# A Mamba-2 scan on one NeuronCore: the state part of y from C scaled per head

## What is computed

```python
cb = einsum('bclgn,bcsgn->bclsg', Cm, Bm)
wts = cb[..., None] * decay * dt[:, :, None]
y_diag = einsum('bclsgr,bcsgrp->bclgrp', wts, x)
...
y_off = einsum('bclgn,bcgrpn,bclgr->bclgrp', Cm, h_prev, exp(acum))
y = (y_diag + y_off).reshape(b, L, SSD_HEADS, P)
```

## Time and profile before

| | us |
|---|---|
| median of 3 runs | 1295.1 |
| lowest, highest | 1293.67, 1297.56 |
| the profiled execution | 1294.7 |
| its span, first to last instruction | 1293.0 |
| PE busy | 1199.7 (93%) |
| DVE, ACT, POOL busy | 522.7, 410.7, 428.1 |
| mean granted clock of PE, share of full speed | 0.973 |

### The profile page before, as it was taken

One profiled execution on the slowest core, in us unless ns is written; L12 is line 12 of the kernel. 1 busy time (PEld: TensorE's weight loads), 2 busy tenths in 40 slices (PEclk: granted clock), 3 DMA queues, 4 the chain that ended last, 5 costly groups with the idle time before them and its releaser, 6 DMA issues.

```text
span 1293.0 us, 22479 instructions
## 1 busy us (share of the span) xinstructions
PE 1199.7 (93%) x8759; PEld 1040.4 (80%) x8759; DVE 522.7 (40%) x855; ACT 410.7 (32%) x690; POOL 428.1 (33%) x343
## 2 busy tenths in 40 slices
PE   5999999999998999999899999999997879887985
PEld 5999999999985997798698689999997645543542
DVE  5445442101645665484665561104344241130114
ACT  4211214343444454453444452222324100010112
POOL 6444432233424432452342343434330111213210
PEclk8999999999999999999999999999999899997999
DMA  6332322123510730451162132253638999999995
GB/s 159 78 82 74 81 78 66 53 82 82 147 50 18 189 82 17 119 135 50 53 169 66 33 106 72 76 136 108 204 106 310 387 401 403 407 402 392 403 370 173
DMA packets 185911, 207.51 MB, mean 160 GB/s; under 512 B 12781, under 2 KB 162669, under 8 KB 177354
## 3 DMA queue, kind: packets, MB, share of 16 engines
q1 hardware_dynamic: 175962, 187.42, 43.8%
q0 software_dynamic: 6048, 12.54, 3.5%
q10 hardware_dynamic: 3822, 6.39, 1.3%
HBM read 191.71 MB, written 26.20 MB: 169 GB/s over the span
## 4 chain that ended last, share of the span: by engine, by line
PE 80%; DMA 8%; DVE 4%; issue 3%; POOL 2%; ACT 2%; SPq 1%; ACTq 0%; DVEq 0%; POOLq 0%
PE acc L677 52%; PE pTS L1076 6%; PE acc L959 4%; PE acc L1120 3%; DMA area<-in_w_down 2%; DMA area<-in_w_up 2%; DMA ring<-in_w_gate 2%; PE pTS L859 2%; PE pY L853 2%; PE pY L877 1%; SPq L602 1%; PE pO L807 1%; PE acc L818 1%; DMA area<-in_w_down,area 1%; PE pO L827 1%
## 5 line engine op out<-in xcount | busy, mean ns | idle before, releaser
L677 PE MATMUL acc<-h_parts,ring_parts 128*128 128x328 f32 (+1 forms) x3840 | 543.1, 303 | 6.3 <-DVE area L1340 2.2
L677 PEld LDWEIGHTS acc<-h_parts,ring_parts 128*128 128x128 f32 x3840 | 532.3, 190 | 18.2 <-issue 11.5
L1993 POOL TENSOR_TENSOR ring_parts<-ring,ring_parts 128x1024 fp32r<-128x1024 f32 x112 | 280.8, 2507 | 494.2 <-ACT ring_parts L1691 494.1
L1691 ACT ACTIVATE ring_parts<-ring 128x1024 fp32r<-128x1024 f32 x112 | 118.8, 1060 | 379.5 <-PE acc L677 352.7
L1076 PE MATMUL pTS<-area,big 128*64 128x256 f32 x672 | 108.4, 406 | 17.9 <-DMA ring<-in_w_gate 6.2
L677 PE MATMUL acc<-u_parts,ring_parts 128*128 128x264 f32 (+1 forms) x640 | 109.4, 299 | 0.0
L1076 PEld LDWEIGHTS pTS<-area,big 128*64 128x64 f32 x672 | 68.2, 147 | 51.0 <-issue 12.5
L677 PEld LDWEIGHTS acc<-u_parts,ring_parts 128*128 128x128 f32 x640 | 96.4, 188 | 0.0
L677 PE MATMUL acc<-area_parts,ring_parts 128*128 128x264 f32 (+1 forms) x512 | 91.1, 299 | 0.0
L1296 DVE SCALAR_TENSOR_TENSOR area<-area,xvec 128x616 f32<-128x616 f32 x72 | 79.4, 1102 | 10.5 <-DVE area L1294 0.6
L677 PEld LDWEIGHTS acc<-area_parts,ring_parts 128*128 128x128 f32 x512 | 78.4, 188 | 0.0
(11 more groups left out here) (397 smaller groups left out, 1519.5 us busy)
## 6 DMA issues: line engine op xcount, KB each, us to landing
ring<-in_w_in SPq DMA_DIRECT2D x80, 512.0 KB, 4.0
area<-in_w_gate SPq DMA_DIRECT2D x20, 1024.0 KB, 20.9
area<-in_w_up SPq DMA_DIRECT2D x20, 1024.0 KB, 22.9
area<-in_w_down SPq DMA_DIRECT2D x20, 1024.0 KB, 21.2
area<-in_state_ssm SPq DMA_DIRECT2D x16, 512.0 KB, 6.9
out<-area SPq DMA_DIRECT2D x16, 512.0 KB, 5.4
ring<-in_w_ssd_out SPq DMA_DIRECT2D x16, 512.0 KB, 4.1
ring<-in_w_gate SPq DMA_DIRECT2D x7, 1024.0 KB, 16.8
```

The costliest lines, as they stand in the source:

```text
L677: m = nc.tensor.matmul(acc[a][:, h, 0:n], w[s][:, k, :], x[:, k, h * HALF:h * HALF + n], start=first and k == 0 and w is w_hi and x is hi, ...
L1691: a_.activation(w_hi[b % 2], w_raw[b % 2], ACT.Copy).then_inc(hi_done, 1)
L1993: gp.tensor_tensor(w_lo[b % 2], w_raw[b % 2], w_hi[b % 2].bitcast(F32), ALU.subtract).then_inc(lo_done, 1)
```

## The change

In tiles 0 to 3 the state part is no longer made with tokens on the partitions and turned back. C (128 state rows by 128 tokens) is multiplied by `exp(acum)` once per head, and eight matmuls, one per head, add state times these features right into `pY`, ahead of the batch with the weights. The factors lie along the tokens, so they have to stand on all 128 partitions: ACT makes `e_row` = exp of the running sums (32 heads by 592) once, SP writes it to DRAM (`e_rows`, one row per full tile), and in each full tile ACT issues two DMAs which read 512 numbers of a row (4 heads by 128 tokens) to all partitions, into `c_of`, in the place of the convolution's `raw` buffers. POOL then multiplies C in (`scale_c`) and signals PE (`s_ce`). L807, L1328 and L877 remain in tile 4 alone.

The core of the diff (in the full one `z_y` and `p_yo` give up their semaphores, and counts follow):

```diff
+        e_row = area[0:HEADS, at_pad + T:at_pad + 2 * T]
+        c_of = [raw[:, n, XH:XH + 4 * P] for n in range(2)]
+        e_rows = nc.dram_tensor("e_rows", [4, HEADS * P], F32).ap()
 # SP, ahead of the scan
-            sp.wait_ge(s_dta, 8)
+            sp.wait_ge(s_dta, 9)
+            for i in range(4):
+                sp.dma_start(e_rows[i].rearrange("(h c) -> h c", c=P), e_row[:, i * P:(i + 1) * P]).then_inc(ac_rows, 16)
...
-            sp.wait_ge(ac_rows, 32)
+            sp.wait_ge(ac_rows, 96)
 # PE
-                    pe.wait_ge(s_y1, g * 5 + (i + 1))
+                    if i == 0:
+                        pe.wait_ge(s_y1, g + 1)
+                    else:
+                        pe.wait_ge(s_cb, g * 5 + i)
+                        pe.wait_ge(s_bt, g * 5 + i)
...
-                    pe.wait_ge(s_cb, g * 5 + (i + 1))
-                    pe.wait_ge(s_bt, g * 5 + (i + 1))
-                    if i < 4:
-                        nc.tensor.matmul(pO[0:r, :], cT[:, tok(i)], st, start=True, stop=True).then_inc(p_yo, 1)
...
+                    pe.wait_ge(s_exp, g * 10 + (2 * i + 3))
+                    if i < 4:
+                        pe.wait_ge(s_ce, g * 4 + (i + 1))
+                        for h in range(HPG):
+                            half, at = head(h)
+                            nc.tensor.matmul(pY[half, at], st[:, h * HD:(h + 1) * HD], c_of[h // 4][:, h % 4 * P:(h % 4 + 1) * P],
+                                             start=h < 2, stop=False)
...
-                    pe.wait_ge(s_y1, g * 5 + (i + 2))
-                    for k in range(GK):
...
 # DVE
-                        dve.wait_ge(p_yo, g * 4 + (i + 1))
+                        dve.wait_ge(p_y, g * 5 + (i + 2))
...
-                    dve.wait_ge(p_yt, g * 5 + (i + 1))
+                    if i == 4:
+                        dve.wait_ge(p_yt, g + 1)
 # ACT, once, and in each tile between the copy of B and the exps
+            a_.activation(e_row, xT_new[0:HEADS, 0:T], ACT.Exp).then_inc(s_dta, 1)
...
+                    if i < 4:
+                        act.wait_ge(s_cvd, g * 6 + 8)
+                        act.wait_ge(ac_rows, 96)
+                        for q in range(2):
+                            act.dma_start(c_of[q], e_rows[i:i + 1, bass.ds(g * (HPG * P) + q * 4 * P, 4 * P)].broadcast_to([P, 4 * P])
+                                          ).then_inc(e_in, 16)
 # POOL
+                def scale_c(i):
+
+                    hold(pool, e_in, g * 128 + (32 * i + 32))
+                    for q in range(2):
+                        by_head = c_of[q].rearrange("p (h c) -> p h c", h=4)
+                        x = gp.tensor_tensor(by_head, by_head, cT[:, tok(i)].unsqueeze(1).broadcast_to([P, 4, P]), ALU.mult)
+                    x.then_inc(s_ce, 1)
+
+                hold(pool, s_silu, g * 6 + 8)
+                scale_c(0)
                 split_lo(g_block(g, 6), 6)
                 for i in range(1, TILES):
                     if i < 4:
+                        scale_c(i)
                         split_lo(g_block(g, 6 + i), 6 + i)
```

More of the change, by code:

```diff
@@ L329, in build @@
         s_hist, s_tail, s_cvd, s_silu = (sem(n) for n in ("s_hist", "s_tail", "s_cvd", "s_silu"))
-        p_xt, p_cb, p_seg, p_yo, p_y, p_sn, p_yt = (sem(n) for n in ("p_xt", "p_cb", "p_seg", "p_yo", "p_y", "p_sn", "p_yt"))
+        p_xt, p_cb, p_seg, e_in, p_y, p_sn, p_yt = (sem(n) for n in ("p_xt", "p_cb", "p_seg", "e_in", "p_y", "p_sn", "p_yt"))
         s_u, s_y1, s_xd, s_cb, s_bt, s_ac, s_exp, s_w, s_st = (
@@ L362, in build @@
                              "f_out", "f_skip"))
-        z_sd, z_y, y_out = (sem(n) for n in ("z_sd", "z_y", "y_out"))
+        z_sd, s_ce, y_out = (sem(n) for n in ("z_sd", "s_ce", "y_out"))
         def s_block(turn, b):
@@ L649, in _ @@
             for i in range(TILES):
-                sp.wait_ge(z_y, i + 1)
+                sp.wait_ge(s_htok, TILES + i + 1)
                 if i == 0:
@@ L792, in _ @@
                         if q == 0:
[L793 removed]
+                            pe.wait_ge(ac_rows, 96 + 16 * TILES * (g + 1))
                             pe.wait_ge(s_exp, g * 10 + (2 * i + 1))
@@ L851, in _ @@
                     for h in range(HPG):
-                        k, half = h // 2, slice(HD * (h % 2), HD * (h % 2) + HD)
-                        m = nc.tensor.matmul(pY[half, k * P:k * P + r], xdt[0:r, i % 2, h * HD:(h + 1) * HD],
-                                             wts[0:r, h // 4, (h % 4) * r:(h % 4 + 1) * r], start=h < 2, stop=False)
+                        half, at = head(h)
+                        m = nc.tensor.matmul(pY[half, at], xdt[0:r, i % 2, h * HD:(h + 1) * HD],
+                                             wts[0:r, h // 4, (h % 4) * r:(h % 4 + 1) * r], start=i == 4 and h < 2,
+                                             stop=i < 4 and h >= HPG - 2)
                     m.then_inc(p_y, 1)
                     kk = r if i < 4 else LASTP
-                    pe.wait_ge(s_exp, g * 10 + (2 * i + 3))
                     nc.tensor.matmul(pS[:, :], btok[0:kk, i % 2, :], xte[0:kk, i % 2, :], start=True, stop=True
@@ L863, in _ @@
                         pe.wait_ge(s_bm, g + 1)
-                        pe.wait_ge(s_y1, g * 5 + 6)
+                        pe.wait_ge(s_y1, g + 2)
                         def state_update(k):
@@ L873, in _ @@
                         state_update(1)
-                    pe.wait_ge(s_y1, g * 5 + (i + 2))
-                    for k in range(GK):
-                        m = nc.tensor.matmul(pY[:, k * P:k * P + r], ytok[0:r, k * P:(k + 1) * P], ident[0:r, 0:r],
-                                             start=False, stop=k == GK - 1)
-                    m.then_inc(p_yt, 1)
+                        pe.wait_ge(s_y1, g + 2)
+                        for k in range(GK):
+                            m = nc.tensor.matmul(pY[:, k * P:k * P + r], ytok[0:r, k * P:(k + 1) * P], ident[0:r, 0:r],
+                                                 start=False, stop=k == GK - 1)
+                        m.then_inc(p_yt, 1)
                 pe.wait_ge(s_st, g * 6 + 6)
@@ L1269, in _ @@
             v.tensor_scalar(da.rearrange("p i h -> p (i h)"), pY[:, 0:160], -1.0, None, ALU.mult).then_inc(s_ac, 1)
-            dve.wait_ge(s_dta, 8)
+            dve.wait_ge(s_dta, 9)
             v.memset(arow.bitcast(F32), 0.0).then_inc(s_ac, 1)
@@ L2080, in _ @@
                     if i < 4:
+                        scale_c(i)
                         split_lo(g_block(g, 6 + i), 6 + i)
                     if i == 1:
-                        hold(pool, s_silu, g * 6 + 8)
                         gp.tensor_copy(cmask[:, 0:LASTP], cT[:, 4 * P:TP])
```

13 lines of the change are left out of this document (8 added, 5 removed).

## The result

The changed kernel takes 1331.0 us (median of 4 runs, 1328.4 to 1332.9) against 1296.3 us before on the same chip, a ratio of 1.027 with a 95% interval of 1.0242 to 1.0298. The forecast was 1308 us with a range up to 1320: the sign is right and the size is not, 35 us instead of 13. The profiled execution took 1331.9 us, 37.2 more than that of before.

What follows compares the result with a forecast made beforehand. PE, busy 93% of the span, was taken as the bound. Tiles 0 to 3 at +1.45, -0.58, -0.58 and +3.0 gave +3.3 us a group, times 4 +13.2, on 1294.7: 1308 us, range 1295.5 to 1320.

Steps and rivals of the forecast that it cites:

- Two batches of 1.02 later: Tile 0: after PE may start at 475.9, two matmul batches of 1.02 us end L853 at 477.94, +1.45 us.
- 2.04 in tile 3's sum: Tile 3: the two batches after the 8.4 us chain, ending at 10.44 against 7.42 before, +3.0 us.
- a lower granted clock: Listed for the scan as a sign that the forecast is wrong, without a size.
- Landing from the first issue: Each full tile: both row transfers landed 3.4 us after the first issue, floor 2.7, ceiling 4.0.
- The two products: Each full tile: GpSimd's two 128x512 products take 2.4 us, plus 0.35 for VectorE in tiles 0 and 3.
- Tiles 1 and 2: New chain hidden with 1.1 us to spare; each tile gains 0.58 us.
- about 2 to 3 us: Sign the forecast is right: PE idles this long before the new matmuls of tiles 0 and 3, released by POOL.
- The start-up: Before the scan: one more ACT activation and four SP issues, put at 0; uncovered 2.2 us, once.
- (c): Rival: 128 copies of one row land late; at 6.0 us landing the kernel takes 1341 us; chance 0.07.
- (a): Rival: new chain just covered, landing 2.7, POOL 1.9, nothing for DVE; 1295.5 us; chance 0.11.
- (b): Rival: the features are never late, -1.36 us a group, 1289.3 us; chance 0.05.
- The meeting of GpSimd and DVE: Tiles 0 and 3: VectorE's weights product beside POOL's multiply adds half a product, 0.35 us, to the chain.

Runs made afterwards that it cites:

- x4: Changed kernel plus 20 (tile 0) and 44 (tile 3) unread matmuls on PE ahead of its wait for GpSimd: 1316.9 us.
- x5: Changed kernel with ScalarE issuing the row transfers earlier, ahead of the copy of B, tile 0's right after the last silu: 1313.4 us.
- x6: Changed kernel with two row buffers, the next tile's rows issued after this tile's exps, tile 0's after the last silu: 1304.4 us.
- x8: x6 with rows asked for at the tile's start, and GpSimd's products and splits held until the previous tile's state is updated: 1302.6 us.
- x3: Changed kernel without row transfers; GpSimd multiplies C with resident ones once the tile before is done, factor exp(acum) left out: 1286.9 us.
- x10: x9 without the holds on GpSimd's products and splits: 1304.2 us.
- x12: x9 with the scan's first split put ahead of tile 0's product on GpSimd, without a hold of its own: 1291.3 us.
- x1: Changed kernel without row transfers, GpSimd's products and PE's wait for them; new matmuls read C itself, factor left out: 1303.1 us.
- x9: x8 with tile 0's rows issued before the last silu, tile 1's after tile 0's exps, last split held for tile 3's state: 1295.6 us.
- x7: x1 with GpSimd's split of a weight block in the scan held until the state of the tile before is updated: 1281.8 us.
- x11: x9 with the scan's first split also held until the state of tile 0 is updated: 1303.8 us.

## Why the prediction was wrong in size

**The step that failed** is "Two batches of 1.02 later", in tile 0, and the 2.04 in tile 3's sum. They were priced from a trace in which PE came to them without a wait (and half a us in the earlier trace rows). Behind the new waits the two batches took 3.46 us in tile 0 (488.34 to the state matmul's start at 491.80) and 3.62 in tile 3 (524.38 to 528.00), and tile 3's state matmuls 0.55 more than before. That is 1.42 + 1.58 + 0.55 = 3.55 us a group, 14.2 in all; in x4, where the clock stayed up, the tiles of the four groups are 14.6 us shorter. The prediction listed a lower granted clock as a sign against it, but gave it neither a price nor a chance. The Trainium skill ("TensorE: Matmul & The Clock Gate", section "The HAM clock gate (the "warmup" mystery)") calls the lower level, 1.2 GHz, the default state, from which activity releases the engine to 2.4. The rows at 0.50 and 1.00 agree, and so does x4, where matmuls that compute nothing keep 1.00.

**The chain's terms.** PE was forecast to start L863 7.45 us into tile 0 and 8.4 after tile 2's last batch; it started at 8.08 and 9.40. Landing from the first issue was put at 3.4 with a ceiling of 4.0. It took 3.74 in tile 0 (481.45 to 485.19) and 4.80 in tile 3 (517.13 to 521.93), where the DMA engines were 87% busy at 240 GB/s. The median of 3.4 is that of each issue; the pair is complete only with the second one, 0.4 later. The prediction counted this 0.4 in its floor (2.7) and not in its ceiling (4.0). The two products were put at 2.4 + 0.35 for the meeting with DVE: 2.84 in tile 0, where they met a decay product (1.16 us instead of 0.69), and 2.14 in tile 3, where they met none. Hand-overs were put at 0.05 and took 0.31 in both tiles. The errors are +0.63 and +1.0 us, 6.5 us over four groups.

**Together**: 13.2 forecast + 14.2 clock + 6.5 chain + about 3 ahead of the scan = 37, against 37.2 between the two profiled executions; smaller errors in tiles 1, 2 and 4 cancel within a us. That this comes out so close is in part luck, since it takes the second group four times. Added up over all twenty tiles the scan lost 35.6 us, the stretch ahead of it 3.0, and some 1.4 came back between the groups and behind them.

**What held.** Tiles 1 and 2 were to gain 0.58 each and gained 0.47; the 11.60 stands in all kernels without a meeting, so it is PE's own sum but for a wait of 0.17. The chain is hidden there, as forecast. The splits on GpSimd came in time: SP's loads waited longer for them (243.6 us in 28 waits of the scan, the longest 15.6, before 195.2 and 11.7), but PE waited for no weight block. Of the signs, "about 2 to 3 us" of idling fits tile 0 (2.62) and not tile 3 (5.67). Tile 4 was put at 0 and lost 0.2, with the end of tile 3's slow state matmuls in it.

**The start-up** was put at 0. The 3 us there are a clock that fell at 307 us with PE busy. All kernels of the experiments have the same start-up code. In x5, x6 and x8 the granted clock stays at 1.00 there; in x3, x4, x10 and x12 it falls for about half as long (x3 0.77 and 0.81 from 303 to 311 us); in x1 and x9 it falls as in the changed kernel (0.65 and 0.50, 0.50 and 0.76 from 307 to 315). So the new transfers do not bring it by themselves; what decides it stays open.

**The rivals.** (c), the slow broadcast, is out: the median landing is 3.4 us. (a) is out, since neither the landing nor the hand-overs were at their floor. (b) is what x3 shows in part: without the transfer the same code is 0.6% faster than before, and without transfer, products and meetings (x7) 1.05%; both leave the factor out. (b) was put at 1289.3 us, close to x3's 1286.9 and 7.5 us above x7's 1281.8.

**The meeting of GpSimd and DVE** was priced at half a product, in tiles 0 and 3 alone. In the changed kernel that was about right, by luck of the order: the products hold the splits back until DVE is done (its product of state and decay takes 693 ns on average there). Where an experiment moved GpSimd, one or the other of DVE's products took longer: state times decay up to three times as long, 2.04 instead of 0.69 (x1), the two decay products 4.18 together instead of 1.4 (x6). The Trainium skill ("SBUF — State Buffer", section "SBUF: two separate sides") calls this an exclusive lock held for a whole instruction; 2.04 is close to the 2.36 of the split less the 0.86 by which it had started earlier, plus DVE's own 0.69 (2.19), so x1 agrees.

## What to carry to other kernels

A wait that a change puts in front of TensorE can have two prices, its own length and the slower work behind it; work out both as a range, since the second came in all eight places of the changed kernel and in one of four in x8. Look at the granted clock of the stretch behind each wait; a wait may be covered with other matmuls even where they compute nothing. A transfer that feeds the bounding engine belongs one tile ahead, in a second buffer, before any sum on its landing time is made. And an instruction of VectorE that a change moves onto the path must be held against what GpSimd runs at that time: one wait on GpSimd made 21 us between x1 and x7, the clock's part included.

## What was not expected of the hardware

- The clock fell from 1.00 to 0.50 around single waits of 2.62 and 5.67 us in the middle of a scan in which PE is otherwise busy, and stayed there while PE worked (tile 3: 0.50 from 525 to 529 us, with PE busy all the time). The length of the wait alone does not decide it: behind x11's 1.81 us the mean was 0.63, behind x8's 2.54 it stayed at 1.00, and x7's waits of 0.17, 0.23 and 1.4 us cost nothing in three groups and slowed the batches in one. What decides it stays open.
- 20 and 44 matmuls that compute nothing, 2.6 and 5.5 us long, made the kernel 14.1 us faster.
- A shorter wait did not always help the clock: 4.03 us instead of 5.67 left the batches at 1.97 and 1.95 us (x5).
- A row of 2 KB sent to 128 partitions lands in 3.4 us, near the 4.0 of a 512 KB weight block, and in 4.4 at most: reading one source row 128 times did not bring the 6 us or more of rival (c).
